# Head rows side by side, the query wave ahead of the projection, and a norm conversion through two PSUM banks

## The reference

```python
xn = rms_norm(x, norm_w)
proj = xn @ w_in                      # many slices of columns
# Mamba-2 branch, 16 heads
dt = softplus(dt_raw + dt_bias); a = -exp(a_log)
a_cum = cumsum(dt * a) within each chunk of 128 positions
y_a = ssd_scan(conv_silu(xbc), dt, a_cum) * silu(z); grouped norm
# sliding-window branch: 16 query heads, 4 kv heads, window 128
q, k = rope(q), rope(k); y_b = softmax(q k^T / 8 with sinks) v * silu(z)
# forgetting branch, 16 heads
cum = cumsum(log_sigmoid(f_logit + f_bias)) over all 512 positions
y_c = softmax(q k^T / 8 + cum_i - cum_j, causal) v * silu(z)
x = x + (sum_b sigmoid(gate_b) * (y_b @ w_proj_b)) @ w_out
```

## Time and profile before

| | before |
|---|---|
| time of three runs, median (lowest to highest) | 3553.54 us (3551.41 to 3555.57) |
| the profiled execution | 3551.3 us, span 3549.5 us |
| TensorE busy, instructions | 3405.1 us, 17054 |
| VectorE busy | 1596.1 us |
| ScalarE busy | 850.6 us |
| GpSimd busy | 2126.0 us |
| mean granted clock of TensorE | 0.992 of full speed |

### The profile page before, as it was taken

The page is one execution under the profiler, slowest core; times in us unless marked ns, Lnnn a source line. Parts: engine busy times, 40 slices in busy tenths (PEclk is TensorE's granted clock), DMA queues, the critical chain, the costliest instruction groups (busy, mean ns, idle before and its releaser), DMA issues.

```text
span 3549.5 us, 49094 instructions
## 1 busy us (share of the span) xinstructions
PE 3405.1 (96%) x17054; PEld 2724.3 (77%) x17054; DVE 1596.1 (45%) x2917; ACT 850.6 (24%) x1717; POOL 2126.0 (60%) x2084
## 2 busy tenths in 40 slices
PE   8999999999999999998999999999989999999998
PEld 6778788877787788876877777777868777777776
DVE  6545542116545521027654552332576545523325
ACT  2223211001232211012213531332122135313321
POOL 7645577767554677664556556445845565564455
PEclk9999999999999999999999999999999999999999
DMA  3212122222221122221212212111212122121121
GB/s 132 94 59 71 65 100 96 95 95 84 72 71 71 72 95 95 103 99 59 82 59 83 80 64 92 63 60 72 98 60 81 59 83 79 65 91 64 60 72 71
DMA packets 39902, 281.22 MB, mean 79 GB/s; under 512 B 4800, under 2 KB 5312, under 8 KB 6336
## 3 DMA queue, kind: packets, MB, share of 16 engines
q1 hardware_dynamic: 38880, 277.96, 22.0%
q10 hardware_dynamic: 864, 1.11, 0.1%
HBM read 276.96 MB, written 2.10 MB: 79 GB/s over the span
## 4 chain that ended last, share of the span: by engine, by line
PE 83%; DVE 9%; ACT 3%; issue 3%; POOL 1%; DMA 0%; DVEq 0%; ACTq 0%; SPq 0%; POOLq 0%
PE banks L363 20%; PE banks L365 19%; PE banks L364 19%; PE banks L614 2%; PE banks L612 2%; PE banks L613 2%; PE banks L916 1%; PE banks L940 1%; PE banks L927 1%; PE banks L406 1%; PE banks L583 1%; PE banks L408 1%; PE banks L407 1%; PE banks L919 1%; PE banks L729 1%
## 5 line engine op out<-in xcount | busy, mean ns | idle before, releaser
L326 POOL TENSOR_SCALAR whi<-raw 128x512 fp32r<-128x512 f32 x1040 | 732.9, 714 | 1389.9 <-PE banks L365 1161.4
L331 POOL TENSOR_TENSOR wlo<-raw,whi 128x512 fp32r<-128x512 f32 x1040 | 1439.0, 1394 | 0.0
L363 PE MATMUL banks<-xhi,whi 128*128 128x512 f32 x2832 | 1163.4, 411 | 49.6 <-POOL wlo L331 19.8
L365 PE MATMUL banks<-xhi,wlo 128*128 128x512 f32 x2832 | 1111.9, 393 | 0.0
L364 PE MATMUL banks<-xlo,whi 128*128 128x512 f32 x2832 | 1109.1, 392 | 0.0
L363 PEld LDWEIGHTS banks<-xhi,whi 128*128 128x128 f32 x2832 | 535.9, 189 | 182.7 <-issue 49.0
L365 PEld LDWEIGHTS banks<-xhi,wlo 128*128 128x128 f32 x2832 | 534.1, 189 | 117.6
L364 PEld LDWEIGHTS banks<-xlo,whi 128*128 128x128 f32 x2832 | 536.3, 189 | 105.9 <-issue 8.1
L363 PE MATMUL banks<-yhi,whi 128*128 128x512 f32 x544 | 217.0, 399 | 17.1 <-DVE ylo L1650 5.6
L364 PE MATMUL banks<-ylo,whi 128*128 128x512 f32 x544 | 213.6, 393 | 0.0
L365 PE MATMUL banks<-yhi,wlo 128*128 128x512 f32 x544 | 213.4, 392 | 0.0
(11 more groups left out here) (286 smaller groups left out, 4591.8 us busy)
## 6 DMA issues: line engine op xcount, KB each, us to landing
raw<-weights SPq DMA_DIRECT2D x260, 1024.0 KB, 4.8
x<-x_in SPq DMA_DIRECT2D x4, 512.0 KB, 8.0
out<-merged SPq DMA_DIRECT2D x1, 2048.0 KB, 6.3
rot<-const SPq DMA_DIRECT2D x1, 512.0 KB, 11.5
rot<-const ACTq DMA_DIRECT2D x1, 512.0 KB, 3.9
wide_mask<-const ACTq DMA_DIRECT2D x1, 384.0 KB, 5.2
wide_mask<-const SPq DMA_DIRECT2D x1, 256.0 KB, 12.1
cst<-const SPq DMA_DIRECT2D x1, 232.0 KB, 9.3
```

The lines of the kernel that those rows point to most:

```text
L326: pool.tensor_scalar(whi[p][:, w], raw[p][:, w], 1.0, 1.0, ALU.mult, ALU.mult).then_inc(s("hi_written"), 1)
L331: return pool.tensor_tensor(wlo[p][:, w], raw[p][:, w], whi[p][:, w].bitcast(F32), ALU.subtract)
L363: pe.matmul(dst, whi[p][:, w], hi[:, k, :], start=start and i == 0, stop=False)
L365: mm = pe.matmul(dst, wlo[p][:, w], hi[:, k, :], start=False, stop=stop and last_k)
```

## The change

1. `raw_norm` writes the scaled tile into PSUM bank 6 or 7, by turns, instead of `merged`; ScalarE and VectorE read it there. From tile 2 on VectorE first waits until its own low part of two tiles before is done. This holds for all six norms.
2. The head rows stay on rows 0 to 15 and 32 to 47 and are treated as one piece of 48 x 512, with a sign and a bias per row. One scan makes both sums; a constant row (`keep`, loaded for each layer) restarts it at chunk borders for dt. The logarithm is done in ScalarE's norm after tile 1, the sums on VectorE after tile 4, and the rounding of the sums (`split_sums`) after the first convolution pair. The layer's setup is done ahead of the first tile.
3. In the second block the sums and the spread of the norm are issued one k step earlier.
4. The query wave of group 0 is issued before the projection, with the tail's two steps between and behind its halves, into banks 2 and 3. ScalarE copies kv rows and queries, and VectorE rotates them, before the projection is read out; the turned v is made after the third projection wave. The second query half is rotated through a tile of its own.

```diff
@@ -250,10 +250,17 @@
...
         swa_q, swa_v = (q2[:, 0:3, :], q3), (v2[:, :, 0:64], v2[:, :, 64:128])
+        def swa_rot(g, half):
+            return q3[:, 2, :] if g == 0 and half else rot_q[:, :]
         fox_q = (sg[:, 0:4, :], q2)
...
         spread = sg[:, 7, :]
+        keep = hst[:, :, :].rearrange("p a n -> p (a n)")[0:48, 0:S]
+        rates, log_part = ea[0:48, 0, :], ya[0:48, 0, :]
         cv = merged[:, 0:4, :]
@@ -630,7 +637,7 @@
...
                 raw_waves(L + 2 * DEPTH, base, 0, tiles(DOWN_ORDER),
-                          {(0, 7): lambda: norm_sums(L + 2 * DEPTH, DOWN_ORDER), (1, 2): lambda: norm_spread(L + 2 * DEPTH)})
+                          {(0, 6): lambda: norm_sums(L + 2 * DEPTH, DOWN_ORDER), (1, 1): lambda: norm_spread(L + 2 * DEPTH)})
@@ -755,19 +762,22 @@
...
-                def projection(first, b):
+                start_wave(base + W_Q, 1)
+                tile_product(bank(2), 1, 0, xhi, xlo, range(KT))
+                ssm_tail((L + 1) * GROUPS - 1, 0)
+                tile_product(bank(3), 1, KT, xhi, xlo, range(KT)).then_inc(wave_done, 1)
+                ssm_tail((L + 1) * GROUPS - 1, 1)
+                def projection(first, b, between=None):
                     def ready(k):
-                        if b == 0 and k in (1, 4):
-                            ssm_tail((L + 1) * GROUPS - 1, k // 3)
                         if k == KT - 2:
...
                     for i in range(4):
-                        wave_t(first + i, (i + (b == 0)) % 2, yhi, ylo, ready if i == 0 else None)
-                pe.wait_ge(s("y_split"), (3 * L + 1) * GROUPS - 1)
-                projection(base + W_PA, 0)
+                        wave_t(first + i, i % 2, yhi, ylo, ready if i == 0 else None)
+                        if i == 2 and between is not None:
+                            between()
@@ -842,12 +852,10 @@
...
+                pe.wait_ge(s("y_split"), (3 * L + 1) * GROUPS - 1)
+                projection(base + W_PA, 0, lambda: swa_turn_v(0))
                 pe.wait_ge(drained[0], swa + 4)
-                start_wave(swa + 1, 1)
-                pe.wait_ge(s("swa_read"), L * GROUPS + 1)
-                tile_product(bank(0), 1, 0, xhi, xlo, range(KT))
-                swa_turn_v(0)
-                tile_product(bank(1), 1, KT, xhi, xlo, range(KT)).then_inc(wave_done, 1)
+                pe.wait_ge(drained[1], swa + 4)
                 swa_fill(0, 0, KT)
@@ -1035,7 +1043,7 @@
...
                         act.wait_ge(wave_done, second)
-                    copy_hi(xhi[:, t, :], merged[:, t, :], "norm_hi")
+                    copy_hi(xhi[:, t, :], bank(6 + t % 2), "norm_hi")
                     if t in between:
@@ -1136,28 +1144,29 @@
             act.wait_ge(s("x_out"), DEPTH + 1)
-            act.dma_start(rot[:, :, :], const[:, C_C2:NC_].rearrange("p (a n) -> p a n", a=2)).then_inc(s("rot2"), 16)
+            act.dma_start(rot[:, :, :], const[:, C_C2:C_KEEP].rearrange("p (a n) -> p a n", a=2)).then_inc(s("rot2"), 16)
             act.dma_start(wide_mask[:, :], const[:, C_WM2:C_C1]).then_inc(s("rot2"), 16)
...
                 act.dma_start(par[:, 0:NP2], par2[L]).then_inc(s_par, 16)
+                act.dma_start(keep, const[0:48, C_KEEP:C_KEEP + S]).then_inc(s_par, 16)
                 own.begin()
-                def head_exp():
-                    act.wait_ge(s_par, 16 * (L + DEPTH + 1))
+                def head_log():
+                    act.wait_ge(s_par, 32 * (L + 1) + 16 * DEPTH)
                     own(act.activation(lamc[0:16, 0:1], par[0:16, R_ALOG:R_ALOG + 1], ACT.Exp))
-                    act.wait_ge(s("head_abs"), L + 1)
-                    own(act.activation(ya[0:16, :, :], ya[0:16, :, :], ACT.Exp, scale=-1.0))
-                def head_log():
-                    own.done()
-                    own(act.activation(ya[0:16, :, :], ya[0:16, :, :], ACT.Ln, bias=1.0))
+                    act.wait_ge(s("head_logits"), L + 1)
+                    own(act.activation(log_part, rates, ACT.Abs))
+                    own.done()
+                    own(act.activation(log_part, log_part, ACT.Exp, scale=-1.0))
+                    own.done()
+                    own(act.activation(log_part, log_part, ACT.Ln, bias=1.0))
                     own.done()
...
                 spread_out(L + 2 * DEPTH)
-                norm(L + 2 * DEPTH, base + 2, {4: head_exp, 5: head_log})
+                norm(L + 2 * DEPTH, base + 2, {1: head_log})
@@ -1269,11 +1278,11 @@
...
                     own(act.activation(swa_q[g % 2][:, half, :], bank(b), ACT.Copy))
-                    if g or half:
+                    if g:
                         act.wait_ge(s("swa_roped"), 3 * (L * GROUPS + g) + 2 * half)
...
                         source = 32 * (c ^ 1)
-                        own(act.activation(rot_q[32 * c:32 * c + 32, :], psum[source:source + 32, b, :], ACT.Copy))
+                        own(act.activation(swa_rot(g, half)[32 * c:32 * c + 32, :], psum[source:source + 32, b, :], ACT.Copy))
                     own.done()
@@ -1301,13 +1310,14 @@
...
+                apart(act)
+                swa_kv_out(0, kv_first[:, :])
+                act.wait_ge(wave_done, base + W_Q + 1)
+                swa_q_out(0, 0, 2)
+                swa_q_out(0, 1, 3)
+                swa_v_out(0)
                 act.wait_ge(s_proj[0], L + 1)
                 apart(act)
-                swa_kv_out(0, kv_first[:, :])
-                swa_v_out(0)
-                act.wait_ge(wave_done, swa + 2)
-                swa_q_out(0, 0, 0)
-                swa_q_out(0, 1, 1)
                 swa_half_out(0)
@@ -1433,21 +1443,25 @@
...
-            def raw_norm(it, between):
+            def raw_norm(it, between, early=None):
...
                 diagonals(sg[:, 0, :], root).then_inc(s("norm_diag"), 1)
+                if early is not None:
+                    early()
                 dve.wait_ge(s("spread_out"), it + 1)
...
                     dve.wait_ge(s("norm_hi"), KT * it + t + 1)
-                    dve.tensor_tensor(xlo[:, t, :], merged[:, t, :], xhi[:, t, :].bitcast(F32), ALU.subtract)\
+                    dve.tensor_tensor(xlo[:, t, :], bank(6 + t % 2), xhi[:, t, :].bitcast(F32), ALU.subtract)\
                        .then_inc(s("norm_split"), 1)
                 for t in range(KT):
-                    dve.scalar_tensor_tensor(merged[:, t, :], x[:, t, :], gains[:, bass.ds(KT * it + t, 1)], bank(5),
+                    if t >= 2:
+                        dve.wait_ge(s("norm_split"), KT * it + t - 1)
+                    dve.scalar_tensor_tensor(bank(6 + t % 2), x[:, t, :], gains[:, bass.ds(KT * it + t, 1)], bank(5),
                                              ALU.mult, ALU.mult).then_inc(s("norm_scaled"), 1)
@@ -1744,65 +1758,59 @@
...
                 base = L * N2 + DEPTH * N1
-                eb = ea[0:16, :, :]
-                yr = ya[0:16, :, :]
...
                     dve.wait_ge(wave_done, base + 1)
-                    own(dve.tensor_tensor(eb[:, 0, :], psum[0:16, 0, :], spread[0:16, :], ALU.mult))
-                    own(dve.tensor_tensor(eb[:, 1, :], psum[32:48, 0, :], spread[32:48, :], ALU.mult))
+                    own(dve.tensor_tensor(rates, psum[0:48, 0, :], spread[0:48, :], ALU.mult))
+                    dve.wait_ge(s_par, 32 * (L + 1) + 16 * DEPTH)
+                    own.done()
+                    own(dve.tensor_scalar(rates, rates, par[0:48, R_HB:R_HB + 1], par[0:48, R_SIGN:R_SIGN + 1], ALU.add, ALU.mult))
+                    own.done()
+                    dve.nop().then_inc(s("head_logits"), 1)
...
-                def head_abs():
-                    dve.wait_ge(s_par, 16 * (L + DEPTH + 1))
-                    for a, c in enumerate((R_DTB, R_FB)):
-                        own(dve.tensor_scalar(eb[:, a, :], eb[:, a, :], par[0:16, c:c + 1], None, ALU.add))
-                    own.done()
-                    own(dve.scalar_tensor_tensor(yr, eb, -1.0, eb, ALU.mult, ALU.max))
-                    own.done()
-                    dve.nop().then_inc(s("head_abs"), 1)
-                raw_norm(L + 2 * DEPTH, {1: first_heads, 3: head_abs})
+                def head_sums():
+                    dve.wait_ge(s("head_log"), L + 1)
+                    own(dve.tensor_scalar(lamc[0:16, 1:2], lamc[0:16, 0:1], -1.0, None, ALU.mult))
+                    own(dve.scalar_tensor_tensor(log_part, rates, 0.0, log_part, ALU.max, ALU.add))
+                    own.done()
+                    own(dve.tensor_scalar(rates, log_part, lamc[0:48, 1:2], None, ALU.mult))
+                    own.done()
+                    own(dve.tensor_tensor_scan(cbs[0:48, :], keep, rates, 0.0, ALU.mult, ALU.add))
+                    own.done()
+                    dve.nop().then_inc(s("head_rows"), 1)
+                def head_columns():
+                    dve.wait_ge(s("head_cols"), L + 1)
+                    own(dve.tensor_copy(cols[:, :, :, :].rearrange("p a c h -> p (a c h)"), psum[:, 4, 0:128]))
```

(60 more changed lines are left out.)

28 lines of the change are left out of this document (11 added, 17 removed).

## The result

The changed kernel takes 3545.84 us (median of 14 runs, 3541.90 to 3548.16), the kernel before on the same chip 3555.48 us (14 runs, 3551.41 to 3561.95). The ratio is 0.9972 with an interval of 0.9964 to 0.9979: 7 to 13 us faster, forecast 8.6. Its page begins like this; TensorE was busy 3404.0 us of it, before 3405.1, with the same number of instructions: of the 8.6 us, 7.5 are less idle time of TensorE and 1.1 less busy time.

A forecast was written before the change was run, and what follows sets the result against it. TensorE, busy 96% of the span, bounds the kernel, so only its waits or slow clock pay. 3551.3 - 9.0 (part 2) + 0.4 (part 1) = 3542.7, with the median 2.2 higher 3544.9; forecast 3540 to 3550, with rivals 3535 to 3553.

The forecast's parts named there:

- part 1: Second block's norm, heads and conversion through PSUM: +4.4 us from an earlier convolved tile, -4.8 for slow clock, together -0.4 us.
- part 2: Query wave before the projection, second block: 6.0 us gained less 1.5 for slow clock per layer, +9.0 us in two layers.
- The wait moves: Second block's norm: the 7.12 us wait at the transposes becomes more than 8 us at the first turned tile.
- the rival by which this wait was the one that counted: Wait at the transposes (L642) goes and nothing takes its place: 3520 us; chance 0.04.
- First tile to last low part: VectorE's chain in the second block's norm, from first scaled tile to last low part: 21.4 us instead of 19.0.
- Last low part to convolved tile: VectorE's chain from the norm's last low part to the first convolved tile: 16.5 us instead of 20.45.
- The slow clock: TensorE at half speed behind the wait at the first turned tile: costs 1.7 to 3.0 us, taken as 2.4 per layer.
- The new wait: TensorE waits 4.0 us per layer before the second projection wave for banks 2-3, which ScalarE empties; 1.5 charged for slow clock.
- The projection's read: VectorE's three rotations come before it; banks 0-1 are free at 1871.6, wanted at 1876.8: hidden, by 5 us.
- The norms of the first block: The first block's four norms also go through PSUM; TensorE has no wait for a low part there: 0.
- VectorE meets GpSimd nowhere: Rival: in the second block's norm and head sums VectorE never meets GpSimd, clock back after 3.4 us: 3536; chance 0.2.
- Given back: Rival: clock 3.0 instead of 2.4, head sums and split as long as bounded: 3552.7, no difference; chance 0.16.

The follow-up runs named there:

- part 1 alone: Kernel before with only points 1 to 3 (norm through PSUM, head rows as one piece, sums and spread one k step earlier): 3555.17 us, ratio 1.0002.
- part 2 alone: Kernel before with only point 4, the query wave of group 0 ahead of the projection: 3546.24 us, ratio 0.9978.
- no_detour: Changed kernel with the scaled tiles back in merged instead of PSUM and without VectorE's six waits for itself: 3552.81 us, ratio 0.9992.
- detour_first: Changed kernel with the normed tile through PSUM only in the first block's four norms, the second block's two through merged: 3549.51 us, ratio 0.9987.
- keep_busy: Changed kernel with 30 extra matmuls of 512 columns per layer in TensorE's wait at the first turned tile, adding nothing to the result: 3539.55 us, ratio 0.9957.
- both moves: Changed kernel with the split of the sums behind the fourth convolved tile and ScalarE's query copies ahead of the kv rows: 3523.05 us, ratio 0.9913.
- second block only: Changed kernel with the normed tile through PSUM only in the second block's two norms: 3546.14 us, ratio 0.9976.

## Why the prediction came out right, and where it was off

**The sum.** Forecast 3544.9, measured 3545.84; 8.6 us less in the profiled execution, as forecast. That the profile meets the 8.6 is luck: part 1 is -0.4 forecast and -1.0 in the profile, part 2 +9.0 and +6.7, so 5.7 together, and the other 2.83 us are clock in the first block that no step of mine foresaw. The runs, which average over such stretches, give 9.6 us; part 1 alone gives nothing there and part 2 alone 8.6 by the medians (5 to 11), so by the runs the parts came out as forecast too.

**The wait moves.** Right. The 7.12 us wait is gone, and 3.75 in the wave at the fifth k step (forecast 3 to 5, there) and 7.90 at the turned tile (forecast over 8, and 7 to 9 among the signs) stand in its place. Part 1 alone measures no gain, and the rival by which this wait was the one that counted (3520) is out.

**First tile to last low part.** Forecast 21.4, measured 20.2 in the first layer and 20.85 in the second. The low part of tile 2 began 8.75 us behind the first tile where the sum has 9.6, since the heads and ScalarE's logarithm took less. The scan took 2.16 instead of 1.21, in this and every other kernel that has it, with GpSimd at work for all of it or for half of it alike (no kernel ran it with GpSimd idle): so its form costs that rather than GpSimd (the old one was add and minimum against a repeated constant on 16 rows, the new one is multiply and add with a stored row on 48; which of these costs it wasn't tried). The head sums took 3.9 all the same, within their bounds of 2.9 to 6.5. A pair of tile and low part came every 1.49 us with the new wait (forecast 1.45) and every 1.26 without it and without PSUM (no_detour), so the wait for itself costs some 0.2 for a pair, twice the 0.1 that I charged.

**Last low part to convolved tile.** Forecast 16.5, measured 18.8. Two terms were too small. The split of the sums, 3.6 forecast in bounds of 2.1 to 4.9, took 4.95: it fell into GpSimd's split of a wave (1617.2 to 1625.4). And I had VectorE never wait for the turned head rows; it waited 1.2, because TensorE comes to them behind its own 3.75 us wait and at half speed. Both chains together are 39.0 in the first layer, against 37.9 forecast and 39.5 before: the tile came 0.5 earlier instead of 1.4. In the second it came 1.1 earlier instead of 3.0. The start was 1.3 earlier there, nearly as forecast, but the chain behind it has the same 18.8 and a first part of 20.85, so it was no shorter than before.

**The slow clock.** Forecast 2.4 per layer. By positions it took 1.3: in the first layer a tile that comes 0.5 earlier turns into 0.8 lost, in the second 1.1 earlier into 0.1 lost. So the step's direction was right and its size nearly twice what it took. Keeping TensorE busy there gives 1.5 us per layer back by positions and 3 in the runs. The two misses of part 1, a tile that comes less early and a clock that costs less, nearly cancel: 4.4 - 4.8 forecast, 1.6 - 2.6 in the profile.

**Part 2.** The new wait came where forecast, released by ScalarE, 3.53 us for 4.0. Behind it 5 us of work ran at half speed, a loss of 2.5 where I charged 1.5: that is the term of part 2 that was mis-sized, and with it 3.1 to 3.5 per layer are left of 4.5 in the profile. Moving the kv rows behind the queries takes that wait away and brings 12 us, so the reason is shown. The projection's read stayed hidden: VectorE's rotations ended at 1867.3, and the bank pair was wanted well behind that.

**The norms of the first block.** Forecast 0; the intervals can't tell it from 0 (detour_first). The detour as a whole I priced at slightly less than nothing (its waits for itself) except through the 0.69 for a low part; in the new layout it is worth 7 us, a good part of it in the second block. I had its mechanism in the price (0.69 throughout instead of up to 1.7) and never summed what its absence would cost.

**The rivals.** That VectorE meets GpSimd nowhere (3536) is out: the split took 4.95. *Given back* (3552.7) needed the clock, the head sums and the split all at their bounds; only the split was, and the clock took 1.3 where that rival has 3.0.

**What stays open.** The detour's measured worth is 3.6 us alone, where a profile shows none of it, and 7 in the new layout, where a profile shows 3.2 in the second block. The same holds for keep_busy (6 us against 3). One guess is that the rest is clock, at places that change from execution to execution. Nothing was run that shows it, and the mean clock over the runs speaks on both sides: after 0.990, without the detour 0.989, both moves 0.993, but before 0.990 in three of its four groups of runs, and part 2 alone and second block only 0.989, although they are as fast as after. The first block may hold some of it. In the 13 profiles, one execution each, the second block starts at 1576.5 to 1583.2 us in the four kernels without the detour in the first block (mean 1579.6) and at 1573.6 to 1581.1 in the nine with it (mean 1576.6). These ranges overlap, and second block only is as fast as after in spite of it, so this is a hint and not shown.

## What to carry to other kernels

When a long wait is removed, follow the chain of the engine that releases the *next* wait: here it hardly moved, and the 14 us of waits that went brought nothing. Work that keeps TensorE from running dry is the gain, and what it needs next (here two banks behind the kv rows, a split ahead of a tile that is wanted sooner) is where the next 23 us were. Two vector operands in SBUF beside a busy GpSimd are dear, so put such an operation where GpSimd rests, or give it one operand in PSUM.

## What the runs showed of the hardware that was not expected

- A multiply-and-add scan of 48 x 512 with a stored row of factors took 2.16 us in each of the ten kernels that have it; the add-and-minimum scan before, on 16 rows, took 1.21 for 512 columns.
- Subtractions of 128 x 512 with both inputs in SBUF took 1.15 and 1.70 us beside GpSimd, the same with one input in PSUM 0.69. Over all norms of a kernel the longest beside GpSimd took 1.71 (mean 1.25) with both inputs in SBUF and 0.69 with one in PSUM. Four operations on 16 x 512 took 4.95 us beside GpSimd and 2.29 away from it.
- The work at half speed does not follow the length of the wait: about 3 us of it behind 7.9 us of waiting, about 5 us behind 3.5. In after the clock had fallen 3.6 us ahead of the end of the long wait, while TensorE stood still, and 1.3 us ahead of the end of the short one (0.64 from 1862.0 to 1863.7), so less of the slow stretch was left behind the long wait:

```profile
1627.00:1630.00 3.00, 0.00 (x0) 0.00 (x0) 1.83 (x4) 2.04 (x5) 0.00 (x0) 0.50 0.78 328
1863.80:1869.00 5.20, 5.20 (x12) 4.08 (x13) 4.93 (x5) 0.00 (x0) 5.20 (x5) 0.50 0.00 0
```

- In the first block, which part 2 alone has instruction for instruction as before, windows lay at 0.54, 0.71 and 0.79 of the clock in one of the two profiles and at another value in the other: part 2 alone shows 0.54 where before has 0.71, and 1.00 where before has 0.79:

```profile
795.00:799.00 4.00, 2.69 (x6) 2.15 (x7) 3.97 (x4) 1.85 (x3) 4.00 (x4) 0.54 0.06 20
1163.00:1167.00 4.00, 2.90 (x17) 2.25 (x16) 3.61 (x5) 1.20 (x2) 4.00 (x4) 1.00 0.00 0
```
